# A two-block transformer kernel on one core: zero matmuls and halved first chunk at the head, GpSimd and fewer transfers at the tail

## The reference

```
h = rms_norm(x, norm_mix[0])                 # x / sqrt(mean(x*x) + eps) * gain
z = h @ pa_w_in[0]                           # the first product
...
return rms_norm_2(x, final_g_2).astype(in_dtype)   # the last normalisation
```

## Time and profile before

| what | us |
|---|---|
| median of 3 runs (1161.2, 1161.66, 1168.12) | 1161.66 |
| the profiled execution | 1161.85 |
| its span | 1160.0 |
| first matmul starts | 11.24 |
| last matmul of the last column starts | 1149.07 |

### The profile page before, as it was taken

How to read it: one execution, slowest core, us unless ns; L and a number is a source line. 1 busy time by engine, 2 the same in 40 slices (tenths; PEclk the granted TensorE clock), 3 DMA queues, 4 the chain that set the end, 5 groups by cost and what they waited for, 6 DMA issues and landing times.

```text
span 1160.0 us, 21002 instructions
## 1 busy us (share of the span) xinstructions
PE 1091.7 (94%) x8588; PEld 1036.3 (89%) x8588; DVE 835.9 (72%) x1444; ACT 641.7 (55%) x1098; POOL 66.7 (6%) x79
## 2 busy tenths in 40 slices
PE   6996999999999979999999989899999979999996
PEld 6874999999987779999999978799989979999996
DVE  6465898887795397978787768998874587655442
ACT  6544576665564975756565675222333357875340
POOL 1130100000002001000000000000000011000010
PEclk9998999999999979999999989999999989999998
DMA  9366465556665844776776533222335255556551
GB/s 344 120 203 235 128 213 185 184 171 180 193 215 186 276 133 135 247 237 228 237 220 185 195 111 107 83 92 91 128 109 155 70 207 179 182 183 183 184 160 37
DMA packets 59857, 200.41 MB, mean 173 GB/s; under 512 B 6769, under 2 KB 11505, under 8 KB 59633
## 3 DMA queue, kind: packets, MB, share of 16 engines
q1 hardware_dynamic: 58032, 194.54, 51.7%
q10 hardware_dynamic: 1728, 4.53, 1.1%
HBM read 197.99 MB, written 1.05 MB: 172 GB/s over the span
## 4 chain that ended last, share of the span: by engine, by line
PE 81%; DVE 10%; ACT 6%; DMA 1%; issue 1%; ACTq 0%; SPq 0%; POOL 0%; DVEq 0%
PE ps L470 80%; DVE wlo L1552 2%; ACT whi L1037 1%; ACT L1037 1%; DVE xr L1558 1%; DMA ring<-pa_w_out 1%; DMA ring<-pa_w_in 1%; ACT xr L1037 1%; DVE cosT L1552 1%; ACT rr L1037 0%; DVE rst L1581 0%; DVE raw L1552 0%; DVE bks L1552 0%; DVE hl L1552 0%; ACT sc L1037 0%
## 5 line engine op out<-in xcount | busy, mean ns | idle before, releaser
L470 PE MATMUL ps<-hh,whi 128*128 128x256 f32 (+1 forms) x1656 | 481.1, 291 | 18.1 <-DVE wlo L1552 15.6
L470 PE MATMUL ps<-hh,wlo 128*128 128x256 f32 (+1 forms) x1656 | 471.3, 285 | 0.0
L470 PE MATMUL ps<-hl,whi 128*128 128x256 f32 (+1 forms) x1656 | 469.4, 283 | 0.0
L1552 DVE TENSOR_TENSOR wlo<-ring,whi 128x1024 fp32r<-128x1024 f32 (+1 forms) x313 | 376.1, 1216 | 73.8 <-ACT whi L1037 73.2
L1037 ACT ACTIVATE whi<-ring 128x1024 fp32r<-128x1024 f32 (+1 forms) x313 | 321.6, 1039 | 68.7 <-PE ps L470 52.6
L470 PEld LDWEIGHTS ps<-hh,whi 128*128 128x128 f32 x1656 | 316.6, 191 | 39.0 <-issue 31.2
L470 PEld LDWEIGHTS ps<-hl,whi 128*128 128x128 f32 x1656 | 317.1, 192 | 1.3 <-issue 1.0
L470 PEld LDWEIGHTS ps<-hh,wlo 128*128 128x128 f32 x1656 | 316.7, 191 | 0.0
L470 PE MATMUL ps<-hidh,whi 128*128 128x256 f32 x608 | 172.2, 283 | 0.0
L470 PE MATMUL ps<-hidh,wlo 128*128 128x256 f32 x608 | 172.1, 283 | 0.0
L470 PE MATMUL ps<-hidl,whi 128*128 128x256 f32 x608 | 172.1, 283 | 0.0
(11 more groups left out here) (360 smaller groups left out, 1354.3 us busy)
## 6 DMA issues: line engine op xcount, KB each, us to landing
ring<-ffn_w_in SPq DMA_DIRECT2D x88, 512.0 KB, 3.5
ring<-ffn_w SPq DMA_DIRECT2D x64, 512.0 KB, 4.4
ring<-w_in SPq DMA_DIRECT2D x51, 512.0 KB, 3.4
ring<-ada_w SPq DMA_DIRECT2D x48, 512.0 KB, 4.3
ring<-ffn_w_out SPq DMA_DIRECT2D x32, 448.0 KB, 3.3
ring<-rg_w_in SPq DMA_DIRECT2D x20, 512.0 KB, 4.4
ring<-pa_w_in SPq DMA_DIRECT2D x16, 512.0 KB, 7.5
ring<-ffn_w_out SPq DMA_DIRECT2D x16, 512.0 KB, 3.6
```

Of the source, the lines that this page charges most:

```text
L470: return e.matmul(o, l, r, start=start, stop=stop)
L1552: return e.tensor_tensor(o, a, b, op)
```

## The change

At the head: VectorE clears `raw[0]`, and TensorE runs 8 float32 matmuls on it, into a bank that nobody reads, ahead of its wait for `ones_in`. The first chunk comes in two transfers of 256 KB, with signals of their own, and ScalarE, VectorE and TensorE take it in halves. ACT issues `cst[:, 0:384]` and the rest of `vec` after both halves of the first chunk's split, and no longer first of all. At the tail: ScalarE multiplies tiles 6 and 7 by `final_g` before it takes the root, GpSimd multiplies them by `rst`, VectorE does tiles 0 to 5, and SP sends pairs of tiles, 4 transfers of 256 KB.

```diff
@@ tensor_program, linear
-                            low.wait_ge(e, c)
+                            low.wait_ge(e, c if c or q > 3 else "half")
@@ tensor_program, start
+            at_dve.wait_ge(e, "zeros")
+            for i in range(8):
+                mm(ps[7][:, 0:T], raw[0][:, 0:128], raw[0], True, True)
             ones_in.wait_ge(e, "all")
@@ scalar_program, feed
-                        act(whi[j % NS][:, 0:nk, :], ring[n % NR][:, 0:nk, :], ACT.Copy).then_inc(*high.up(n))
+                        if n == 0:
+                            act(whi[0][:, 0:4, :], ring[0][:, 0:4, :], ACT.Copy).then_inc(*high.up("half"))
+                            landed_late.wait_ge(e, "all")
+                        k = 0 if n else 4
+                        act(whi[j % NS][:, k:nk, :], ring[n % NR][:, k:nk, :], ACT.Copy).then_inc(*high.up(n))
@@ scalar_program, start
             e.dma_start(vec[:, 0:32], d["vec"][:, 0:32]).then_inc(*gains_in.up("all", 16))
-            e.dma_start(cst[:, 0:384], d["cst"][:, 0:384]).then_inc(*ones_in.up("all", 16))
-            e.dma_start(vec[:, 32:], d["vec"][:, 32:]).then_inc(*vecs_in.up("all", 16))
...
                 if m == 3:
                     feed(-1 - AHEAD)
+                    e.dma_start(cst[:, 0:384], d["cst"][:, 0:384]).then_inc(*ones_in.up("all", 16))
+                    e.dma_start(vec[:, 32:], d["vec"][:, 32:]).then_inc(*vecs_in.up("all", 16))
@@ scalar_program, end
+            square.wait_ge(e, (6, 7))
+            for k in (6, 7):
+                act(x[:, k, :], x[:, k, :], ACT.Copy, P("final_g", k)).then_inc(*fin_act.up(k))
             stats(6)
@@ vector_program, feed
+                        if n == 0:
+                            high.wait_ge(e, "half")
+                            low_of(wlo[0][:, 0:4, :], ring[0][:, 0:4, :], whi[0][:, 0:4, :]).then_inc(*low.up("half"))
+                        k = 0 if n else 4
                         high.wait_ge(e, n)
-                        low_of(wlo[j][:, 0:nk, :], ring[j][:, 0:nk, :], whi[turn[n] % NS][:, 0:nk, :]).then_inc(*low.up(n))
+                        low_of(wlo[j][:, k:nk, :], ring[j][:, k:nk, :], whi[turn[n] % NS][:, k:nk, :]).then_inc(*low.up(n))
@@ vector_program, start and end
+            e.memset(raw[0], 0.0).then_inc(*at_dve.up("zeros"))
...
-            for k in range(8):
+            for k in range(6):
                 stt(x[:, k, :], x[:, k, :], P("final_g", k), rst[:, :], MUL, MUL).then_inc(*fin.up(k))
@@ gpsimd_program, end
+            mean.wait_ge(e, ("rst", 6))
+            for k in (6, 7):
+                fin_act.wait_ge(e, k)
+                e.tensor_tensor(x[:, k, :], x[:, k, :], rst[:, :], MUL).then_inc(*fin_pool.up(k))
@@ sync_program
-                e.dma_start(dst, src).then_inc(*landed[i].up(n, 16))
-            for m in range(8):
-                fin.wait_ge(e, m)
-                e.dma_start(out[:, m, :], x[:, m, :]).then_inc(*x_out.up("all", 16))
+                if n == 0:
+                    e.dma_start(dst[:, 0:4, :], src[:, 0:4, :]).then_inc(*landed[0].up(0, 16))
+                    e.dma_start(dst[:, 4:, :], src[:, 4:, :]).then_inc(*landed_late.up("all", 16))
+                else:
+                    e.dma_start(dst, src).then_inc(*landed[i].up(n, 16))
+            for m in (0, 2, 4):
+                fin.wait_ge(e, m + 1)
+                e.dma_start(out[:, m:m + 2, :], x[:, m:m + 2, :]).then_inc(*x_out.up("all", 16))
+            fin_pool.wait_ge(e, 7)
+            e.dma_start(out[:, 6:8, :], x[:, 6:8, :]).then_inc(*x_out.up("all", 16))
             x_out.wait_ge(e, "all")
```

More of the change, by code:

```diff
@@ L438, in build @@
         rw_pe, rw_act, rw_dve = signal("rwkv_pe"), signal("rwkv_act"), signal("rwkv_dve")
-        fin = signal("final")
+        fin, fin_act, fin_pool, landed_late = (signal(n) for n in ("final", "final_act", "final_pool", "landed_late"))
         where = {}
@@ L2386, in build @@
                    par_act, par_dve, at_pe, at_act, at_dve, at_pool, gains_in, ff_act, ff_dve, rg_pe, rg_act, rg_dve, rg_pool, mx_act, mx_dve,
-                   sv_act, sv_dve, sg_pe, sg_act, sg_dve, s5_pe, s5_act, s5_dve, s5_pool, rw_pe, rw_act, rw_dve, fin)
+                   sv_act, sv_dve, sg_pe, sg_act, sg_dve, s5_pe, s5_act, s5_dve, s5_pool, rw_pe, rw_act, rw_dve, fin, fin_act, fin_pool, landed_late)
         Signal.dry = True
```

## The result

The changed kernel takes 1165.56 us, the median of 22 runs (1163.37 to 1172.35), against 1161.81 for the kernel before in as many: 3.75 us more, a ratio of 1.0038 with a 95% interval of 1.0025 to 1.0052. It is slower, clear of noise, and above the forecast range's end of 1164.1. The profiled execution took 1164.18, 2.33 above before's 1161.85 and 1.4 under the changed kernel's own median.

What follows compares the result with a forecast made beforehand. TensorE, busy 94% of the span, was taken as the bound, so only head and tail count. Head 0.36, clock 0, tail 0.35 make 0.7: 1162.55 against 1161.85, 1162.35 against the median, lowered to 1162.2; range 1159.8 to 1164.1.

Steps and rivals of the forecast that it cites:

- the landing of the constants: Head: issued at 7.5, landing 4.0 us later, so the first real matmul starts at 11.6, 0.36 later than before.
- Rival (3): Head: constants come much later behind the full weight queue, TensorE starts at 13.3, +2.1; 1164.1 us; chance 0.15.
- C: Theory of the experiments, not of the prediction: the late constants cost the head; no single size.
- The zero matmuls: Head: they end between 6.5 and 8.3, the clock is low again when real work begins; no gain.
- the most that the head can give is 1.6: Head: `row_stats` waits for the squares, summed at 17.4, so its start moves at most from 19.1 to 17.45.
- Rival (1): Head: clock holds or is back early, TensorE starts at 11.6 at 2.4 GHz; -1.6, tail +0.35, 1160.4 us; chance 0.27.
- rival (2): Head and tail: constants by 9.6, gap 1.5 to 3 us, GpSimd doesn't hold VectorE; -1.6 - 0.6, 1159.5 us; chance 0.10.
- one gap only: Head: TensorE idle 3.3 to 5.1 us from the zero matmuls' end to 11.6, taken to lose the clock; no gain.
- The tail: After the reciprocal: GpSimd's two products slow VectorE by 2 x 0.52, the last transfer lands in 2.2; 0.35 us later.
- The chances: Whole kernel, change against about 1% (11.6 us): same 0.97, faster 0.01, slower 0.02.

Runs made afterwards that it cites:

- its head alone: The change's head with the tail of the kernel before; 1164.57 us, 1.0027 to the kernel before.
- no zero matmuls: The changed kernel without its 8 zero matmuls and the clearing of `raw[0]`; 1165.35 us, 1.0028 to the kernel before.
- constants on SP: The changed kernel, but SP issues the 192 KB of constants right behind the first chunk's second half; 1162.84 us, 1.0010 to the kernel before.
- wait at first use: The changed kernel, but TensorE waits for the constants ahead of the sums of squares, not the first column; 1163.15 us, 1.0012 to the kernel before.
- constants first: The changed kernel, but both transfers of constants are issued first of all, as before; 1163.5 us, 1.0018 to the kernel before.
- zero matmuls alone: The kernel before with only the 8 zero matmuls added; 1160.86 us, 0.9994 to the kernel before.
- waits filled: Changed kernel with constants awaited at first use, zero matmuls 11 at start, 2 between columns, 4 ahead of sums, pairs all on VectorE; 1160.19 us, 0.9983.
- wait at first use without zero matmuls: The changed kernel with the constants awaited at their first use and no zero matmuls, the change's tail kept; 1160.07 us, 0.9990 to the kernel before.
- the pairs on VectorE: The kernel before with all eight tail products on VectorE and four transfers of pairs; 1161.16 us, 0.9996 to the kernel before.
- head zeros as changed: Changed kernel with constants awaited at first use, the 8 zero matmuls kept, 2 more between columns and 4 ahead of the sums; 1161.08 us, 0.9994.

## Why the prediction was wrong

**The step that failed is the landing of the constants.** It was put as 4.0 us from issue to landing, of 3.4 to 4.3, with 5.7 as the far end. It took 6.0 in the profile after, and 5.9 to 7.0 in those of the eight experiments that issue it at the same place. The step's mechanism was right, its size was off. (The issue itself came 0.3 later than forecast, 7.79 for 7.5.) I split the 5.9 us of the 704 KB transfer into 2.4 fixed and 3.5 of moving, and took the 2.4 along to a moment at which SP's queue was at its fullest. At 17.7 us, where that row is from, most of those nine chunks had landed, and ACT's queue moved its first packet after some 1.7 us; at 7.8 nearly all of them stood ahead, and it took 3.4. My far end, 5.7, was itself a row of another moment. The first matmul so came at 13.87 to 14.74, 2.6 to 3.5 us later and not 0.36. Rival (3) had the mechanism, at 0.15, with 13.3 for its start and 1164.1 for its time.

**What the median is made of.** Over the three profiles with the late wait (the change, its head alone, no zero matmuls) the first real matmul starts at 14.27 on average, 3.0 after 11.24; with the tail's 0.5 that is 3.5 of the 3.75 measured. In the pair of profiles alone it is 2.3 at attention's first wait (38.05 against 35.73) and 0.5 of the tail; the missing 0.5 is between the two, where stretches at the half clock fall differently: before had one from 50.1 to 53.4, the changed profile has none there. That this sum comes so near the 3.75 is partly luck. From attention's wait to the reciprocal, a stretch whose chain no edit touches, the sixteen profiles take from 1115.1 us (constants first) to 1119.9 (zero matmuls alone), a spread larger than the whole loss. What holds C up are the medians: 2.7, 2.4 and 2.1 us came back when only the constants' place or the wait for them was moved (constants on SP, wait at first use, constants first).

**The zero matmuls** were put at nothing, and that fits the change's median: 1165.35 without them. The reason was as given, a gap too long for the clock (7.5 us instead of 3.3 to 5.1). What I had not seen is that they can cost: once the real work starts early, a column at the full clock is through before the next low part and before the squares, and idle stretches follow, behind which the clock stood at 0.50 for 6 us of work in the profiles of two kernels. The forecast's "the most that the head can give is 1.6" held to 0.1: attention's wait ended 1.60 to 1.63 sooner in the profiles of waits filled and of wait at first use without zero matmuls. The 1.6 was reached by taking them out, as well as by adding more. Rival (1), the clock held at 11.6, and rival (2) were not what happened.

**The Trainium skill's page** "TensorE: Matmul & The Clock Gate", Part 1, was used for one gap only. That idleness is the way back to the throttled state, as it says, fits the later waits in direction: the window from 18.5 to 24.4 reads 0.50 behind waits of 2.33, 0.89 and 1.84 us, and 1.00 behind a single one of 1.51. How much idleness it takes these traces don't settle. Behind a first wait of 1.90 (constants first) the clock was down within 1 us of work, behind one of 1.86 (constants on SP) it stayed up until about 17.7.

**The tail** was put at +0.35 and is +0.5. VectorE's six products were to take 3.4 to 3.5 and took 3.49, 1.0 more than six alone would. GpSimd's two took 1.59 together and both ended ahead of VectorE's second, where I had them in turn; so the first transfer left at 1157.62, later than I had it, and the last at 1159.58, 3.9 us behind the reciprocal's end, where I had 4.0. What I had too short is the stretch from that issue to the end of the span: 2.8 us, against 2.35 before, so 0.45 more where I allowed 0.2. Of that, 2.4 are its landing; it was issued 0.38 behind the transfer before it, where the pairs on VectorE are issued 0.79 apart and land in 2.1. That the closeness makes the difference is likely, but was not tested. ScalarE's two products cost nothing: its root starts 0.02 behind VectorE's row, with 0.31 us to spare.

**The chances** of a change below 1% were right (0.97). The forecast had the sign and a seventh of the size: 0.54 above the median of before, where it is 3.75.

## What to carry to other kernels

Look at where the wait for a thing stands before its transfer is moved back: the first use may be 8 us later than the wait, and one line moves the wait there. Price a late transfer by the queue that it will meet at that moment, not by a row from a quieter one. Starting an engine early, or fast, is worth only what its suppliers can follow; where they can't, the idle time can cost more than the start gained. Here doing less (no zero matmuls, no GpSimd, 1159.91) was as fast as filling every wait (1160.19). And look where among a kernel's runs the profiled one lies before its rows are taken for the median's cause.

## What the runs showed of the hardware

A transfer of 192 KB on ACT's queue, issued at 7.8 us or so while SP's queue of weights was deep, took 5.9 to 7.0 us, in the changed kernel with no packet moved in the first 3.4; on SP's own queue, issued at 2.6 ahead of most of them, 5.6.

Matmuls on zeros do raise the granted clock. The first real one took 0.36 us where they had ended 0.33 us before (waits filled) up to 2.33 (wait at first use), and 0.55 at a clock of 0.50 without any, or with 3.8 us of idle time behind them (zero matmuls alone).

And a fall of the clock was not tied to one long idle stretch. Three waits of 0.5 to 2.3 us within 12 us were followed by 6 us at 0.50 in two kernels (wait at first use, constants on SP), and a single one of 1.90 by 3.2 us at 0.50 in a third (constants first). In the six where the waits were filled or only one was left, none followed up to 36 us, though one of them had a first wait of 2.23 (head zeros as changed). How each wait contributes I could not tell from one profile of each kernel.
